# Attention's output normalised ahead of its split, its sum over partitions behind the third pair's fifth product, the MLP norm's sum as two rounded parts

## What is computed

```
merged = concat([rmsnorm(o, attn_out_g), rmsnorm(y_lru, lru_out_g)])   # each group of 512 columns has its own norm
h = x + merged @ w_out
f = square(relu(rmsnorm(h, norm_mlp_g) @ w_up)) @ w_down
return h + f
```

## Time and profile before

| | us |
|---|---|
| median of three runs (lowest, highest) | 2448.15 (2447.86, 2449.62) |
| the profiled execution, its own time | 2447.68 |
| its span, from the first to the last instruction | 2445.8 |
| PE busy in the span | 2433.3 (99%) |
| DVE busy | 1807.5 (74%) |
| ACT busy | 1285.5 (53%) |
| POOL busy | 538.2 (22%) |

### The profile page before, as it was taken

One profiled execution on the slowest core, in us unless ns is written; L12 is line 12 of the kernel. 1 busy time (PEld: TensorE's weight loads), 2 busy tenths in 40 slices (PEclk: granted clock), 3 DMA queues, 4 the chain that ended last, 5 costly groups with the idle time before them and its releaser, 6 DMA issues. The chain is left out here.

```text
span 2445.8 us, 44404 instructions
## 1 busy us (share of the span) xinstructions
PE 2433.3 (99%) x17454; PEld 2350.6 (96%) x17454; DVE 1807.5 (74%) x2893; ACT 1285.5 (53%) x2306; POOL 538.2 (22%) x513
## 2 busy tenths in 40 slices
PE   9999999999999999999999999999999999999998
PEld 9999977899999999999999999779999999999998
DVE  8677767778776677677686777677787766776676
ACT  5566355655554454455535763557455544554454
POOL 0024255200112211220201142542002112111213
PEclk9999999999999999999999999999999999999999
DMA  4232200453447634663831221005435456546655
GB/s 164 71 115 73 53 11 20 87 155 106 95 86 140 129 84 98 134 119 87 224 101 52 61 73 53 11 20 110 137 109 111 87 119 132 108 87 122 132 101 188
DMA packets 109741, 242.50 MB, mean 99 GB/s; under 512 B 15536, under 2 KB 18960, under 8 KB 109408
## 3 DMA queue, kind: packets, MB, share of 16 engines
q0 software_dynamic: 48512, 102.26, 23.3%
q1 hardware_dynamic: 60880, 137.37, 18.0%
q10 hardware_dynamic: 144, 0.04, 0.0%
HBM read 147.39 MB, written 94.29 MB: 99 GB/s over the span
## 5 line engine op out<-in xcount | busy, mean ns | idle before, releaser
L3233 DVE TENSOR_TENSOR wlo<-raw_all,whi 128x512 fp32r<-128x512 f32 (+1 forms) x420 | 270.2, 652 | 182.1 <-ACT whi L2271 179.6
L2271 ACT ACTIVATE whi<-raw_all 128x512 fp32r<-128x512 f32 (+1 forms) x420 | 248.6, 599 | 280.5 <-DVE raw_all L3366 88.5
L3755 POOL DMA_DIRECT2D x_scratch<-stage x224 | 200.0, 943 | 838.9 <-DVE stage L3376 693.8
L2324 ACT ACTIVATE stage<-ps 128x536 f32<-128x536 f32 (+1 forms) x224 | 135.4, 612 | 146.8 <-PE ps L1554 142.7
L3376 DVE TENSOR_TENSOR stage<-stage,ps 128x536 f32<-128x536 f32 (+1 forms) x168 | 118.9, 708 | 84.7 <-PE ps L1554 83.7
L2836 DVE TENSOR_REDUCE mxp<-ps 128x1 f32<-128x80 f32 (+10 forms) x376 | 139.2, 376 | 54.0 <-PE ps L1270 46.8
L1079 PE MATMUL ps<-xgh,whi 128*128 128x358 f32 (+1 forms) x720 | 157.2, 326 | 0.0
L1079 PE MATMUL ps<-xgl,whi 128*128 128x358 f32 (+1 forms) x720 | 156.6, 325 | 0.0
L1079 PE MATMUL ps<-xgh,wlo 128*128 128x358 f32 (+1 forms) x720 | 156.5, 325 | 0.0
L1702 ACT ACTIVATE whi<-raw_all 128x1024 fp32r<-128x1024 f32 (+3 forms) x64 | 58.1, 908 | 175.4 <-PE ps L1079 157.9
L1079 PEld LDWEIGHTS ps<-xgl,whi 128*128 128x128 f32 x720 | 124.0, 189 | 0.0
(11 more groups left out here) (948 smaller groups left out, 7791.0 us busy)
## 6 DMA issues: line engine op xcount, KB each, us to landing
raw_all<-in_wst SPq DMA_DIRECT2D x237, 256.0 KB, 3.4
raw_all<-in_wst SPq DMA_DIRECT2D x74, 512.0 KB, 3.6
x_scratch<-stage POOLq DMA_DIRECT2D x120, 268.0 KB, 6.0
x_scratch<-stage POOLq DMA_DIRECT2D x120, 264.0 KB, 5.9
xall<-x_scratch SPq DMA_DIRECT2D x32, 537.0 KB, 8.4
x_scratch<-xall POOLq DMA_DIRECT2D x24, 537.0 KB, 3.3
raw_all<-in_wst POOLq DMA_DIRECT2D x30, 256.0 KB, 4.7
xall<-in_xT SPq DMA_DIRECT2D x8, 537.0 KB, 8.6
```

What stands on the lines that cost most here:

```text
L2271: nc.scalar.activation(dst, src, ACT.Copy).then_inc(S["u_hi"], 1)
L2324: nc.scalar.activation(quarters(stage_of(L, g, i, n)[:, 0:N2]), src, ACT.Copy, scale=-1.0 if row else 1.0).then_inc(S["x_copy"], 1)
L3233: V.tensor_tensor(dst, src, hi.bitcast(F32), ALU.subtract).then_inc(S["u_lo"], 1)
L3755: pool.dma_start(x_scr[2 * i + row, :, a:b], stage_of(L, g, i, n)[:, 0:b - a], accum_op=ALU.add).then_inc(S[done], 16)
```

## The change

Three things are done. Attention's output `o` is multiplied by `rs` itself (`o_normal`, a new step on DVE, four times) before it is split, so the eight results of OO need no `scaled`: DVE adds them to `x` straight from PSUM. For this `rs` must be there earlier: the squares and their additions move up on ACT and DVE, `invert(3)` and `divide(3)` move up on DVE, SUM_O's six matmuls move on PE from behind the fourth pair's P7 to behind the third pair's P7, Ln and Exp move up on ACT, and the high and low parts of `o` move down. Third, the sum of the MLP norm is made of two rounded parts like the others: ACT copies `xss` rounded into `xss_hi`, DVE makes `xss_lo`, and PE runs six matmuls in place of three in fp32.

The diff, without the renaming of semaphores and buffers:

```
 PE
                     if name == "P1":
+                        if p == 3:
+                            w("root", SUM_O)
...
-                        if (p, name) == (NYP - 1, "P7"):
+                        if (p, name) == (2, "P7"):
                             w("sum_lo", SUM_O)
-                            w("y_add", y_added(p, "P2"))
-                            w("y_copy", y_copied(p - 1, "P4"))
+                            w("y_add", y_added(2, "P2"))
+                            w("y_copy", y_copied(1, "P4"))
                             sum_of_parts(SUM_O, osqt_r, osq_r)
...
-                pe.wait_ge(S["xm_sum"], L * PER["xm_sum"] + 7)
-                sum_of_squares(SUM_MLP, xss)
+                w("sum_lo", SUM_MLP)
+                sum_of_parts(SUM_MLP, xss_hi, xss_lo)
 ACT
                 def o_high(j):
-                    w("o", j + 1)
+                    w("o_n", j + 1)
...
                     w("res_add", 8)
+                    w("xm_sum", 7)
+                    nc.scalar.activation(xss_hi[:, A0:TOK], xss[:, A0:TOK], ACT.Copy).then_inc(S["sum_hi"], 1)
                     copy_out(at, 0, True)
 DVE
+                def o_normal(j):
+                    w("rstd", SUM_O)
+                    w("o_sq", j + 1)
+                    V.tensor_tensor(live(o[j]), live(o[j]), live(rs), ALU.mult).then_inc(S["o_n"], 1)
...
-                    scaled(U_OO + i, osqt, rs, "oo_ev", LIVE)
-                    w("oo_ev", i + 1)
                     w(f"x_in{m}", 32)
-                    V.tensor_tensor(live(x[m]), live(x[m]), live(osqt), ALU.add).then_inc(S["res_add"], 1)
+                    w("mm", U_OO + i + 1)
+                    V.tensor_tensor(chunks(x[m], LIVE), chunks(x[m], LIVE), slot(U_OO + i, LIVE), ALU.add).then_inc(S["res_add"], 1)
...
-                for name, kk in F_ORDER[2:]:
+                for name, kk in F_ORDER[2:4]:
+                    seven_sum(name, kk)
+                w("sum_hi", SUM_MLP)
+                lo(xss_lo[:, LIVE[0]:TOK], xss[:, LIVE[0]:TOK], xss_hi[:, LIVE[0]:TOK], "sum_lo")
+                for name, kk in F_ORDER[4:]:
                     seven_sum(name, kk)
```

More of the change, by code:

```diff
@@ L250 @@
 for _c in range(8):
[L251 removed]
+    READ[U_OO + _c] = ("res_add", _c + 1)
 for _c in range(10):
@@ L578, in trunk @@
                 seven[name, kk] = [part[:, h * HALF:(h + 1) * HALF] for part in b_in[m]]
+        xss_lo, xss_hi = place("xss_lo", "G", PIECE * 6, TOK, F32R), place("xss_hi", "G", PIECE * 4, TOK, F32R)
         xss, xsq = place("xss", "G", PIECE * 6, TOK), [place(f"xsq{n}", "G", PIECE * (2 + 2 * n), TOK) for n in range(2)]
@@ L682, in sum_rest @@
             if n in (SUM_O, SUM_MLP):
-                return ps[:, 1 if n == SUM_O else 5, CH:CH + b - a - SUM_END]
+                return ps[:, 5, CH:CH + b - a - SUM_END]
             return ps[:, 3 * slot_of(sum_at(n, layer)) + 2, CH:CH + b - a - SUM_END]
@@ L2055, in _ @@
                 y_copy(0, "P1")
-                o_high(0)
+                o_square(0)
                 y_copy(0, "P5")
@@ L2059, in _ @@
                 y_copy(0, "P6")
-                o_square(0)
+                o_square(1)
                 y_fill_hi(1, 1)
-                o_high(1)
-                o_square(1)
                 y_copy(0, "P4")
@@ L2067, in _ @@
                 y_fill_hi(1, 3)
+                o_square(2)
                 y_copy(1, "P5")
@@ L2070, in _ @@
                 y_copy(1, "P6")
-                o_high(2)
                 y_fill_hi(2, 1)
-                o_square(2)
+                o_square(3)
                 y_fill_hi(2, 2)
+                w("o_sum", 3)
+                nc.scalar.activation(live(osqt_r), live(osq), ACT.Copy).then_inc(S["sum_hi"], 1)
                 y_copy(1, "P4")
@@ L2077, in _ @@
                 y_copy(2, "P1")
-                o_high(3)
                 y_copy(2, "P5")
@@ L2081, in _ @@
                 y_copy(2, "P6")
-                o_square(3)
                 y_fill_hi(3, 1)
+                log_sum(SUM_O, rs, ATT)
+                exp_root(SUM_O, rs)
                 y_fill_hi(3, 2)
@@ L2086, in _ @@
                 y_fill_hi(3, 3)
+                o_high(0)
                 y_copy(3, "P1")
-                w("o_sum", 3)
-                nc.scalar.activation(live(osqt_r), live(osq), ACT.Copy).then_inc(S["sum_hi"], 1)
+                o_high(1)
                 y_copy(3, "P5")
@@ L2092, in _ @@
                 y_copy(3, "P6")
-                log_rstd(SUM_O, rs, ATT)
+                o_high(2)
+                o_high(3)
                 split(B_OO + 1)
@@ L3028, in _ @@
                 y_add(0, "P3")
-                o_low(0)
+                o_add(1)
                 y_fill_lo(1, 2)
                 y_block_sum(2, 0)
-                o_add(1)
                 y_fill_lo(1, 3)
+                o_add(2)
                 y_fill_lo(2, 0)
                 y_block_sum(2, 1)
-                o_low(1)
+                divide(3)
                 y_add(1, "P2")
@@ L3040, in _ @@
                 y_block_sum(2, 2)
+                o_add(3)
+                y_add(1, "P3")
                 y_block_sum(2, 3)
-                y_add(1, "P3")
-                divide(3)
                 y_fill_lo(2, 2)
+                sum_lo(osq_r, osq, osqt_r, SUM_O)
                 y_block_sum(3, 0)
-                o_add(2)
                 y_fill_lo(2, 3)
@@ L3055, in _ @@
                 y_block_sum(3, 3)
-                o_add(3)
                 y_add(2, "P3")
+                o_normal(0)
                 y_fill_lo(3, 2)
+                o_normal(1)
                 y_fill_lo(3, 3)
-                o_low(3)
-                sum_lo(osq_r, osq, osqt_r, SUM_O)
+                o_low(0)
+                o_normal(2)
                 split(B_OO)
+                o_normal(3)
                 y_add(3, "P2")
                 y_add(3, "P7")
+                o_low(1)
                 y_add(3, "P3")
+                o_low(2)
+                o_low(3)
                 split(B_OO + 1)
@@ L3131, in _ @@
                 for i, m in enumerate(OO_ORDER):
-                    if i == 0:
-                        w("rstd", SUM_O)
                     if i == 6:
```

25 lines of the change are left out of this document (13 added, 12 removed).

## The result

The changed kernel takes 2454.17 us (median of 17 runs, 2452.93 to 2455.16), the kernel before 2448.50 (17 runs, 2446.90 to 2450.71): +5.7 us, a ratio of 1.0023 with a 95% interval of 1.0016 to 1.0029. Forecast were 2452.7 us, in a range of 2449.6 to 2456.5.

The account below looks back on a forecast made before the run. PE, busy 99% of the span, was taken as the bound, so other engines' work counts only where PE waits. Terms −0.7 + 3.0 + 2.3 + 0.5 − 0.5 = +4.6 us gave a median of 2452.7 us, range 2449.6 to 2456.5.

Parts of the forecast that it names:

- Term 1: MLP norm's sum, up to the first down-product: about 0.35 us a layer earlier, −0.7 us in all.
- Term 2: Third pair's P6: waits behind the late divide, fill and copies, 1.5 us a layer, +3.0 us in all.
- Term 3: Fourth pair's P6: its copy stands behind Exp and o_high(0), PE waits 1.15 us a layer, +2.3 us in all.
- The sign named for it: PE's waits list: at lines of Y, two waits of 1.2 to 2 us a layer for ACT's stage and ystage copies.
- rival C: Fourth pair's P6: table switch pauses ACT beyond its load, about 1.28 us more wait, twice; 2455.3 us; chance 0.03.
- Term 4: First product of OO: DVE's addition behind the fourth pair's P3 ends 0.2 and 0.3 us late, +0.5 us in all.
- Term 5: Second layer's third product of OO: the late weight block's load gains on PE, −0.5 us, ends −0.9 and +1.0.
- A: Third and fourth pairs' P6: copies behind P1 come in time, so not slower; 2446.9 us; chance 0.10.
- B: Crowded transfers: divide's wait ends 1 us later in both layers, late weight block gains nothing; 2455.3 us; chance 0.14.
- D: Third pair's P6: broadcast lands early, its copy comes in time, only the second wait arises; 2449.8 us; chance 0.06.

## Why the prediction was right

**What bounds the kernel** was read rightly. DVE lost 6.6 us of work, and the time rose, since PE waits for the order of ACT's and DVE's steps and not for their sum.

**Term 1** was −0.26 and −0.29 where −0.35 a layer was forecast. That DVE's queue and not PE's sum sets the first down-product is shown from both sides: the two-part sum alone costs 2.6 us, and two sums of halves out of DVE's way bring the first down-product forward by 0.55 and 0.70 us.

**Term 2** had the right place, chain and releaser, and was too small, 1.5 against 1.81 and 2.10. What was short is where the chain starts. The broadcast was taken as landed at 474.9, its first issue with the longest landing, but the divide needs both transfers. In the kernel before the first issued landed 6.6 us after its issue and the second 7.4 us after 468.1, at 475.5; read so, the same sum gives 2.1. In the changed kernel the second landed at 475.1 and the divide started at 475.22, so a transfer that happened to be 0.4 sooner took back most of the misreading. The chain behind it was right: 8.94 us from the divide to P6 (475.22, 484.16) against 8.89 in the forecast. In the second layer the divide starts about as far behind the start of Y as in the first (17.06 and 17.11 us), but P6 is due sooner there, 23.82 us behind that start in place of 24.23 in the kernel before, since a product has 264 columns in place of 268; the forecast took one layer's dates for both.

**Term 3** was right to 0.1 us, and its chain of 7.11 us lies inside the 7.06 to 7.18 worked out. The sign named for it, a recorded wait of 1.2 to 2 us, came as 0.85 and 0.89, since the page counts idle time from the end of the record before (the last section has the difference). Exp is released by its table load: with one load it started 1.3 us sooner and the wait was gone. Behind the load of 1.28 us nothing more was paid in the new place either (the load at 491.31, Exp at 492.61), and rival C is out. The Trainium skill, ScalarE: Activation LUTs, section What ACT_TABLE_LOAD costs, adds some 1.38 us of drain to each load; no trace of this case shows it. The Trainium skill, ScalarE: Activation LUTs, section Table sets: the hidden batching unit, counts one load for Ln followed by Exp, since one set has both. The trace of the version with one table load agrees, with 0.04 us between the end of Ln's last part and Exp; in the kernels without that edit two loads stand, in the changed one at 488.16 and 491.31.

**Term 4** came as forecast, 0.25 and 0.36. The version with the first high part late shows what it hides: with P6 free, P7 and OO hold PE instead.

**Term 5** had the right sign and came to its outer end, −0.88 against −0.5: the whole wait went. What decides it is when the block lands. In the fourteen profiles PE waits at OO's third product in six of the 28 layers, and these are the six in which ACT's fill of the block, which the landing releases, started 11.1 us or more behind OO's first product; in the other 22 it was 10.4 us or less. In the changed kernel's second layer SP issued the load 2.1 us ahead of that product (1721.75, 1723.82), in the kernel before 0.7 us behind it (1718.05, 1717.35), so the load did gain on PE, as forecast. From issue to fill it also took less, 8.5 us in place of 10.4, and why isn't shown: with x ahead of it in the queue this time ranges from 8.1 to 12.0 us in the second layer, and one profile with the order of the kernel before up to there (the two-part sum with four sums late) has no wait. So part of the −0.88 belongs to the one execution profiled. With the load issued ahead of x, in three profiles, the fill waited in both layers for PE and no longer for the load. The forecast's words that nobody waits for the third pair's pieces were wrong: SP's load of x does, and these weight loads stand behind it.

**The rivals.** A fell: neither copy came in time. B's lateness of 1 us didn't come, only 0.3 and 0.6 of it, and the late block gained in place of losing. C and D fell; D's support was the transfer that landed in 6.6 us, but that was the first of the two, and the divide needs both. The sum was 4.6 where the steps measured came to 5.6: term 2 was 0.9 short, and the 0.3 that term 5 gained beyond its forecast hid part of it; the forecast's range for its own case, 2450.7 to 2454.7, holds the median of 2454.17.

## What to carry to other kernels

On a kernel whose PE is 99% busy a change that takes work from another engine is judged by one question: which step does PE wait for, and what now stands ahead of it in that step's queue. Moving a long step, or one that waits (here for a broadcast, and for Exp), ahead of copies and fills that PE needs soon makes PE wait too, and moving one of the held steps past it only hands the wait to the next product; what helps is to shorten the chain that is late, or to put the waiting step where PE has slack behind it. And a shorter product on PE is worth nothing where the next one waits for a queue on DVE that the edit has just made longer.

## What the runs showed of the hardware

A wait costs PE more than its recorded idle time. These are the last matmuls ahead of the third pair's P6 and P6 itself:

```profile
482.23 0.42 PE L1400 MATMUL ps<-yt11l,whi 128*128 128x268 f32 x2
484.16 0.49 PE L1400 MATMUL ps<-yt20h,whi 128*128 128x268 f32 x2 [1.51 <-ACT stage L1981]
484.49 0.41 PE L1400 MATMUL ps<-yt20h,wlo 128*128 128x268 f32 x2
```

The idle time of 1.51 us is counted from the end of the record before, 482.65. Without the wait P6 would have started 0.25 us behind the last start, at 482.48, since one group starts while the record of the last one still runs (0.42 us long, 0.25 apart). It came 1.68 us after that, and its first two matmuls then took 0.33 to the next start, in place of 0.26 in the kernel before. At the fourth pair's P6 the same working makes 1.01 us of 0.85 (the last start at 495.64, P6 at 496.90), and 0.32 to the next start. That the overlap has to be built up again behind a wait is a reading of these starts; the ends of matmuls in a profile are modelled.

The late weight block shows how far a load's landing can move. In the changed kernel and in the version with one table load SP issued the second layer's x at nearly the same time and the first of the two weight loads behind it at the same 1721.75; ACT's fill, which waited for that load, started 3.5 us apart. First the changed kernel, then the version with one table load:

```profile
1720.90 0.80 SPq L869 DMA_DIRECT2D xall<-x_scratch  x2
1721.75 5.19 SPq L828 DMA_DIRECT2D raw_all<-in_wst  x2
...
1730.25 1.06 ACT L1704 ACTIVATE whi<-raw_all 128x1024 fp32r<-128x1024 f32 x1 [5.96 <-DMA raw_all<-in_wst]
```

```profile
1720.85 0.85 SPq L869 DMA_DIRECT2D xall<-x_scratch  x2
1721.75 3.34 SPq L828 DMA_DIRECT2D raw_all<-in_wst  x2
...
1733.77 1.06 ACT L1704 ACTIVATE whi<-raw_all 128x1024 fp32r<-128x1024 f32 x1 [11.19 <-DMA raw_all<-in_wst]
```

What else was under way at the DMA engines differs between the two, and which of it made the difference wasn't tried.
